# Attention scores as three rounded products from a ring of five key slots, instead of one full fp32 product from a ring of six

## The reference, cut to what matters

```
q, k = rms_norm(q, q_gain), rms_norm(k, k_gain)            # per head
s = einsum('bnqhd,bnkhd->bnhqk', q, k_band) * Dh ** -0.5   # chunk n sees chunks n-8 .. n
s = s + rel_bias(table, q_off, k_off)                      # distance clipped at +-128
s = where(valid, s, finfo.min)
o = einsum('bnhqk,bnkhd->bnqhd', softmax(s), v_band)
```

## Time and profile before

| | us |
|---|---|
| median of three timed runs | 1662.35 |
| the profiled execution, whole | 1657.24 |
| its span, first to last instruction | 1655.4 |
| TensorE busy in the span | 1589.1 (96%) |
| attention phase, from the first instruction to the last of `turn_o` | about 542 |
| one steady tile of attention (tiles 4 to 14) | 32.9 |

### The profile page before, as it was taken

One profiled execution on the slowest core, in us unless ns is written; L12 is line 12 of the kernel. 1 busy time (PEld: TensorE's weight loads), 2 busy tenths in 40 slices (PEclk: granted clock), 3 DMA queues, 4 the chain that ended last, 5 costly groups with the idle time before them and its releaser, 6 DMA issues. The chain is left out here.

```text
span 1655.4 us, 46730 instructions
## 1 busy us (share of the span) xinstructions
PE 1589.1 (96%) x20178; PEld 1297.6 (78%) x20178; DVE 807.3 (49%) x1152; ACT 878.9 (53%) x1833; POOL 518.7 (31%) x370
## 2 busy tenths in 40 slices
PE   6999999999999899999978999999999997999999
PEld 5788888888888788899976877777777775777787
DVE  5344444444444521121236677677676676533432
ACT  6566666666665521222246677677777675223420
POOL 3423121212130022122133466466465465400000
PEclk9999999999999999999998999999999999999999
DMA  6312211112113633533453223223223235286652
GB/s 244 106 61 93 72 58 50 67 60 73 52 50 122 210 110 115 163 97 100 125 161 111 62 77 106 63 76 106 63 77 104 64 98 185 84 303 224 210 176 76
DMA packets 136301, 184.43 MB, mean 111 GB/s; under 512 B 59153, under 2 KB 88337, under 8 KB 135842
## 3 DMA queue, kind: packets, MB, share of 16 engines
q1 hardware_dynamic: 129186, 170.83, 32.0%
q10 hardware_dynamic: 6912, 10.62, 1.8%
HBM read 122.42 MB, written 59.55 MB: 110 GB/s over the span
## 5 line engine op out<-in xcount | busy, mean ns | idle before, releaser
L677 PE MATMUL a_ps_proj<-a_w_hi,a_x_hi 128*128 128x512 f32 x384 | 155.8, 406 | 0.0
L677 PE MATMUL a_ps_proj<-a_w_hi,a_x_lo 128*128 128x512 f32 x384 | 150.2, 391 | 0.0
L677 PE MATMUL a_ps_proj<-a_w_lo,a_x_hi 128*128 128x512 f32 x384 | 149.6, 390 | 0.0
L587 DVE SCALAR_TENSOR_TENSOR a_stage<-a_ps_s,a_new_bias 128x256 f32<-128x256 f32 x64 | 27.2, 424 | 233.2 <-PE a_ps_s L704 233.2
L2481 PE MATMUL r_ps_gate<-gate_w_hi,gate_x_hi 128*128 128x512 f32 x272 | 119.0, 438 | 5.1 <-PEq L66 3.4
L1181 DVE SCALAR_TENSOR_TENSOR j_out<-j_ps,j_rest,j_part 128x512 f32<-128x512 f32 (+2 forms) x45 | 29.0, 644 | 177.4 <-ACT j_last_cols L1125 134.7
L362 POOL TENSOR_TENSOR a_xT<-a_xT,a_row 128x1024 f32<-128x1024 f32 x17 | 40.4, 2375 | 232.1 <-DMA a_row<-scratch_rstd 224.4
L2481 PE MATMUL r_ps_gate<-gate_w_lo,gate_x_hi 128*128 128x512 f32 x272 | 111.7, 411 | 0.0
L470 ACT ACTIVATE a_stage<-a_stage,a_small 128x640 f32<-128x640 f32 (+4 forms) x128 | 95.8, 752 | 0.9 <-DVE a_small L595 0.9
L1055 POOL TENSOR_TENSOR j_v_prev<-j_v_prev,shift_x 128x512 f32<-128x512 f32 x17 | 22.9, 1349 | 230.1 <-DMA j_v_prev<-scratch_v_raw 216.8
L704 PEld LDWEIGHTS a_ps_s<-a_kT,a_qT 64*128 64x128 f32 x592 | 59.8, 186 | 33.1 <-issue 28.0
(11 more groups left out here) (408 smaller groups left out, 4697.6 us busy)
## 6 DMA issues: line engine op xcount, KB each, us to landing
a_xT<-in_x_T SPq DMA_DIRECT2D x17, 512.0 KB, 3.3
scratch_xT<-a_xT SPq DMA_DIRECT2D x17, 512.0 KB, 2.6
raw<-scratch_xT SPq DMA_DIRECT2D x17, 512.0 KB, 5.4
scratch_gates<-r_gate_out SPq DMA_DIRECT2D x34, 256.0 KB, 3.2
z_gate<-scratch_gates SPq DMA_DIRECT2D x17, 512.0 KB, 3.8
a_x<-in_x_prompt SPq DMA_DIRECT2D x16, 512.0 KB, 3.5
o_x<-in_x_prompt SPq DMA_DIRECT2D x14, 512.0 KB, 4.8
out_y_prompt<-o_y SPq DMA_DIRECT2D x14, 512.0 KB, 2.9
```

The lines of the kernel that those rows point to most:

```text
L587: nc.vector.scalar_tensor_tensor(out=out[:, :, OLD:WIN], in0=ps_new, scalar=SCALE, in1=new_bias[:, 2 * c:2 * c + 2, :], op0=ALU.mult, op1= ...
L677: mm = nc.tensor.matmul(ps_proj[:], a[n % 2][:, k, :], w[:, k, g * AW:(g + 1) * AW], start=(k == 0 and i == 0), stop=(k == KT - 1 and i == 2))
```

## The change: what it does

- **Rounded halves.** Queries and keys are split: ScalarE writes a float32r rounding (`qT_hi`, `kT_hi`) where it wrote `qT` and `kT`, and VectorE writes the remainder (`qT_lo` by `qT_rest`, `kT_lo` by `kT_rest`, one pass over 128x512 each per tile). A score is then hi x hi + hi x lo + lo x hi, three float32r matmuls that add up in PSUM.
- **Ring of five.** Keys sit in five slots (`n % 5`) instead of six. Columns of the scores are ordered by slot of the ring, not by age: slots 0 to 2 ("main", 384 columns) in a bank per head, slots 3 and 4 ("side", 256 columns) of both heads in one bank. `ps_newest` now lies in the two main banks.
- **Order of the products.** First half: side of head 0 and main of head 1, three times in turn; then a wait of TensorE for the first half's last side product (`side_scored`); second half: side of head 1 and main of head 0, three times in turn. Tiles 0 to 2 have no side and no such wait.
- **VectorE reads by age.** `bias_and_max` takes the spans in order of age, cut where the ring wraps, where main meets side, and between far (three oldest) and near (two newest): 2 to 4 pieces in tiles 4 to 15 instead of 2. Far pieces add one mask shared by all heads, near pieces a bias per head. `scores` and the newest transposes now both wait for the count of all pieces (`biased`).
- **Waits on the turned bank.** `turn_qk` and `turn_o` write `ps_turn` only after the remainder has been read from it (`qkT_lo_ready`), and `scores` of a tile waits for `kT_rest`.
- **Smaller.** `k_out` is the same memory as the squares `qk_sq_out`, with a wait in `square_qk` for the stored k; the bias is loaded by one DMA, without waiting for a memset; q and k of the sample tile are written as plain float32. VectorE's reading of the first tile's q and k comes ahead of the loop.

```
...
-        ps_old = ps_s[:, 0:2 * OLD].rearrange("p (e n) -> p e n", e=2)
-        ps_new = ps_s[:, 2 * OLD:2 * WIN].rearrange("p (e n) -> p e n", e=2)
-        ps_newest = ps_s[:, 2 * WIN:2 * WIN + 2 * P].rearrange("p (e n) -> p e n", e=2)
+        main_banks = ps_s[:, 0:2 * 512].rearrange("p (e n) -> p e n", e=2)
+        ps_main, ps_newest = main_banks[:, :, 0:MAIN * P], main_banks[:, :, MAIN * P:(MAIN + 1) * P]
+        ps_side = ps_s[:, 2 * 512:3 * 512].rearrange("p (e n) -> p e n", e=2)
...
+        def side_steps(s):
+            return max(s - NP * MAIN, 0)
+
+        def spans(t, a, b):
+
+            found, j = [], a
+            while j < b:
+                slot = (t + 1 + j) % SLOTS
+                n = min(b - j, (MAIN if slot < MAIN else SLOTS) - slot)
+                found.append((j, j + n, ps_main[:, :, slot * P:(slot + n) * P] if slot < MAIN else ps_side[:, :, (slot - MAIN) * P:(slot - MAIN + n) * P]))
+                j += n
+            return found
+
+        def bias_steps(t):
+            lo = first_slot(t)
+            return [spans(t, lo, FIRST_NEAR), spans(t, max(lo, FIRST_NEAR), SLOTS)]
+
+        def biases(s):
+            return sum(NP * sum(map(len, bias_steps(t))) for t in range(s // NP)) + (s % NP and s % NP * sum(map(len, bias_steps(s // NP))))
 
...
             def square_qk(n, g):
                 act.wait_ge(proj_read, 3 * n + g + 1)
                 wait(act, qk_summed, 2 * n + g)
+                wait(act, k_stored, 16 * (n - 12))
                 nc.scalar.activation(qk_sq_out[:], qk[:, g, :], ACT.Square).then_inc(qk_sq, 1)
...
             def read_qT(n):
                 act.wait_ge(qk_turned, 2 * n + 1)
                 wait(act, scored, NP * (n - 1))
-                nc.scalar.activation(qT[n % 2][:], ps_turn[:].rearrange("p (c n) -> p c n", c=NP), ACT.Copy,
-                                     scale=consts[:, QK_GAIN_AT:QK_GAIN_AT + 1]).then_inc(qkT_ready, 1)
+                out = qT_hi[n % 2][:] if n < DEC else qT_sample[:]
+                nc.scalar.activation(out, ps_turn[:].rearrange("p (c n) -> p c n", c=NP), ACT.Copy,
+                                     scale=consts[:, QK_GAIN_AT:QK_GAIN_AT + 1]).then_inc(qkT_hi_ready, 1)
 
             def read_kT(n):
                 act.wait_ge(qk_turned, 2 * n + 2)
-                wait(act, scored, NP * (n - 1))
-                nc.scalar.activation(kT[:, :, n % RING, :], ps_turn[:].rearrange("p (c n) -> p c n", c=NP), ACT.Copy,
-                                     scale=consts[:, QK_GAIN_AT + 1:QK_GAIN_AT + 2]).then_inc(qkT_ready, 1)
+                wait(act, scored, NP * n)
+                out = kT_hi[:, :, n % SLOTS, :] if n < DEC else kT_sample[:, :, n % SLOTS, :]
+                nc.scalar.activation(out, ps_turn[:].rearrange("p (c n) -> p c n", c=NP), ACT.Copy,
+                                     scale=consts[:, QK_GAIN_AT + 1:QK_GAIN_AT + 2]).then_inc(qkT_hi_ready, 1)
 
             def exps(t, c):
...
+            def qT_rest(n):
+                dve.wait_ge(qkT_hi_ready, 2 * n + 1)
+                wait(dve, scored, NP * (n - 1))
+                nc.vector.scalar_tensor_tensor(out=qT_lo[n % 2][:], in0=ps_turn[:].rearrange("p (c n) -> p c n", c=NP),
+                                               scalar=consts[:, QK_GAIN_AT:QK_GAIN_AT + 1], in1=qT_hi[n % 2][:].bitcast(F32),
+                                               op0=ALU.mult, op1=ALU.subtract).then_inc(qkT_lo_ready, 1)
+
+            def kT_rest(n):
+                dve.wait_ge(qkT_hi_ready, 2 * n + 2)
+                wait(dve, scored, NP * n)
+                nc.vector.scalar_tensor_tensor(out=kT_lo[:, :, n % SLOTS, :], in0=ps_turn[:].rearrange("p (c n) -> p c n", c=NP),
+                                               scalar=consts[:, QK_GAIN_AT + 1:QK_GAIN_AT + 2], in1=kT_hi[:, :, n % SLOTS, :].bitcast(F32),
+                                               op0=ALU.mult, op1=ALU.subtract).then_inc(qkT_lo_ready, 1)
+
             def bias_and_max(t, c):
                 s, lo = NP * t + c, first_slot(t)
                 out = probs[s % 2]
                 wait(dve, p_turned, s - 1)
                 dve.wait_ge(scored, s + 1)
-                nc.vector.scalar_tensor_tensor(out=out[:, :, OLD:WIN], in0=ps_new, scalar=SCALE, in1=new_bias[:, 2 * c:2 * c + 2, :],
-                                               op0=ALU.mult, op1=ALU.add).then_inc(new_biased, 1)
-                if lo * P < OLD:
-                    nc.vector.scalar_tensor_tensor(out=out[:, :, lo * P:OLD], in0=ps_old[:, :, lo * P:OLD], scalar=SCALE,
-                                                   in1=old_bias[:, 2 * c:2 * c + 2, lo * P:OLD], op0=ALU.mult,
-                                                   op1=ALU.add).then_inc(old_biased, 1)
-                    dve.wait_ge(old_biased, s + 1 - NP)
-                dve.wait_ge(new_biased, s + 1)
+                masks = far_mask[:].rearrange("p (o n) -> p o n", o=1).broadcast_to([P, 2, FAR])
+                far, near = bias_steps(t)
+                for a, b, product in far:
+                    nc.vector.scalar_tensor_tensor(out=out[:, :, a * P:b * P], in0=product, scalar=SCALE, in1=masks[:, :, a * P:b * P],
+                                                   op0=ALU.mult, op1=ALU.add).then_inc(biased, 1)
+                for a, b, product in near:
+                    nc.vector.scalar_tensor_tensor(out=out[:, :, a * P:b * P], in0=product, scalar=SCALE,
+                                                   in1=near_bias[:, 2 * c:2 * c + 2, a * P - FAR:b * P - FAR],
+                                                   op0=ALU.mult, op1=ALU.add).then_inc(biased, 1)
+                dve.wait_ge(biased, biases(s + 1))
                 nc.vector.tensor_reduce(neg_max[s % 2], out[:, :, lo * P:WIN], AX_X, ALU.max, negate=True).then_inc(max_ready, 1)
 
             def invert(t):
@@ -625,6 +676,8 @@
             for g in range(2):
                 sum_qk(0, g)
...
+            qT_rest(0)
+            kT_rest(0)
...
                 sum_qk(t + 1, 1)
                 scale_qk(t + 1, 1)
+                if t + 1 < DEC:
+                    qT_rest(t + 1)
 
                 bias_and_max(t, 3)
+                if t + 1 < DEC:
+                    kT_rest(t + 1)
             split_shift_w()
...
                 pe.wait_ge(qk_scaled, 2 * n + g + 1)
-                wait(pe, qkT_ready, 2 * n + g)
+                wait(pe, qkT_hi_ready, 2 * n + g)
+                wait(pe, qkT_lo_ready, min(2 * n + g, 2 * DEC))
                 if g == 0:
                     wait(pe, out_ready, n - 2)
                 for c in range(NP):
@@ -692,26 +750,37 @@
...
             def scores(t, c):
                 s, lo = NP * t + c, first_slot(t)
                 if c == 0:
-                    pe.wait_ge(qkT_ready, 2 * t + 2)
+                    pe.wait_ge(qkT_lo_ready, 2 * t + 2)
                     if t == 0:
                         pe.wait_ge(proj_read, 3)
-                wait(pe, new_biased, s)
-                wait(pe, old_biased, s - NP)
+                wait(pe, biased, biases(s))
                 wait(pe, pT_ready, s - 1)
-
-                def product(e, a, b, out):
-                    half, r = slice(e * HD, (e + 1) * HD), ring(t, a)
-                    return nc.tensor.matmul(out, qT[t % 2][half, c, :], kT[half, c, r:r + b - a, :].rearrange("p j n -> p (j n)"),
-                                            start=True, stop=True)
-
-                product(0, SLOTS - 1, SLOTS, ps_new[:, 0, :]).then_inc(new_scored, 1)
-                cut = next((j for j in range(lo + 1, SLOTS - 1) if ring(t, j) == 0), SLOTS - 1)
-                for a, b in ((lo, cut), (cut, SLOTS - 1)):
-                    for e in (1, 0):
-                        if a < b:
-                            product(e, a, b, ps_old[:, e, a * P:b * P])
-                pe.wait_ge(new_scored, s + 1)
-                product(1, SLOTS - 1, SLOTS, ps_new[:, 1, :]).then_inc(scored, 1)
+                slots = min(t + 1, SLOTS)
+                main, side = min(slots, MAIN), max(slots - MAIN, 0)
+                q, k = (qT_hi[t % 2], qT_hi[t % 2], qT_lo[t % 2]), (kT_hi, kT_lo, kT_hi)
+
+                def main_product(e, i):
+                    half = slice(e * HD, (e + 1) * HD)
+                    return nc.tensor.matmul(ps_main[:, e, 0:main * P], q[i][half, c, :], k[i][half, c, 0:main, :].rearrange("p j n -> p (j n)"),
+                                            start=i == 0, stop=i == 2)
+
+                def side_product(e, i):
+                    half = slice(e * HD, (e + 1) * HD)
+                    return nc.tensor.matmul(ps_side[:, e, 0:side * P], q[i][half, c, :], k[i][half, c, MAIN:slots, :].rearrange("p j n -> p (j n)"),
+                                            start=i == 0, stop=i == 2)
+
+                for i in range(3):
+                    if side:
+                        first = side_product(0, i)
+                    main_product(1, i)
+                if side:
```

(27 more changed lines are left out.)

41 lines of the change are left out of this document (25 added, 16 removed).

## The result

The changed kernel takes 1666.76 us (median of 13 runs, 1661.37 to 1669.38), the kernel before 1657.37 (median of 13 runs beside it, 1655.33 to 1662.82). The ratio is 1.0049, with a 95% interval of 1.0037 to 1.0062: slower, as the interval leaves out 1, by an amount at the edge of the 0.5% that the forecast called no change. The profiled execution took 1663.36 us, its span 1661.4 (before 1657.24 and 1655.4).

What follows compares the result with a forecast made beforehand. TensorE's stream was taken to bound the attention phase. Score blocks +4.7 us and remainders at the start +1.5 us gave +6.2 us, from 1662.35 to 1668.5 us (0.37% slower), range 1656 to 1682.

Steps and rivals of the forecast that it cites:

- blocks, tiles 4 to 15: Score blocks on TensorE in tiles 4 to 15: 1.39 us instead of 1.28, 48 times, +5.1 us.
- block, tile 3: Score blocks in tile 3, with a side of 128 columns: 1.31 us against 1.07, four times, +1.0 us.
- blocks, tile 2: Score blocks in tile 2, no side and no wait: 1.06 us against 0.96, +0.4 us.
- blocks, tiles 0 and 1: Score blocks of the first two tiles: 0.69 us in tile 0 (-1.1), 0.79 to 0.80 in tile 1 (-0.7).
- first scores: Start, before the loop: first scores 1.5 us later than 40.04, bounds 0 and 2.2.
- The wait in mid-block: Between block halves, tiles 4 to 15: wait for head 0's side product ends at 0.675 us, 0.22 after its last column.
- The wait is nearly free: Rival, mid-block: next half begins when main of head 1 is done, block 1.24, -1.1 us in all, 1661.3; chance 0.15.
- Load 0.60: Tile 3's block: last side column at 0.378 us, load behind the wait at 0.60, block 1.31.
- Main of head 1 at 0.106, 0.279, 0.452, of head 0 to 0.964: Tile 2's block, no wait: these start times in us for main of head 1, main of head 0 until 0.964, block 1.06.
- The remainders: VectorE's passes, 0.69 us each: covered in the loop; before it, 0.75 with signal after each copy, +1.5 us.
- VectorE as the bound: Rival: pieces cost 0.2 us instead of 0.075, newest transposes come late, +3.6 us on top, 1672; chance 0.13.
- the other steps have the same slack: Newest transposes outside step 1: 0.5 us of transposes in between or step 1's slack (2.00 against 2.06), so no cost.

Runs made afterwards that it cites:

- single product: The changed kernel with one of the three float32r products instead of three, the rest of the scores left out; 1632.75 us in one execution.
- head-by-head kernel: Changed kernel reordered: side and main of head 0, main of head 1, the wait, then side of head 1; 1664.07 us in one execution.
- The run with the waits alone: Kernel before, with tile 0's two remainders computed into places nothing reads and TensorE waiting for them; 1660.06 us, ratio 1.0016.
- The kernel before with the longer wait alone: Kernel before, with the newest transposes waiting for every bias piece of the next step, not the newest slot's alone; 1656.64 us, ratio 0.9992.
- both edits: Changed kernel with main of head 0 ahead of the wait and the first tile's k transposed into the outputs' bank; 1654.09 us, ratio 0.9985.
- first-tile kernel: Changed kernel with the first tile's k transposed into the outputs' bank, not waiting for q's copy and remainder; 1661.24 us, ratio 1.0028.
- the four with k in the outputs' bank: Changed kernel with that k edit alone, plus main of head 0 ahead, plus filled start, plus later x statistics in tile 2: 1661.24, 1654.09, 1652.66, 1651.75 us.
- filled kernel: Changed kernel with main of head 0 ahead, first tile's k in the outputs' bank, and six projection products filling the start's gaps; 1652.66 us, ratio 0.9976.

## Why the prediction was right, and where it was not

The forecast was +6.2 us on the profiled span; the span grew by 6.0, the ratio of all runs says +8.1, and the medians of 13 lie 9.4 apart. The time itself, 1668.5, was only 1.7 too high because the shown median of three lay 5 us above that of 13 runs: a change forecast too small and a base too high cancel. Attention's last score block ends 9.0 us later (529.3, 538.3). That 6.0 is so near 6.2 is luck too: the 9.0 are met by 3.0 behind the phase that no instruction of the change touches. The mechanism of the largest term is right, four smaller ones are not. Term by term, in us:

| term | forecast | trace |
|---|---|---|
| blocks, tiles 4 to 15 | +5.1 | +5.7 |
| block, tile 3 | +1.0 | +1.4 |
| blocks, tile 2 | +0.4 | -0.9 |
| blocks, tiles 0 and 1 | -1.8 | -3.1 |
| first scores | +1.5 | +1.7 |
| low clock behind them | none | +2.5 |
| newest transposes and other gaps, tiles 0 to 3 | 0 | about +1.6 |
| after the attention phase | 0 | -3.0 |

*The wait in mid-block: right, mechanism and size.* Its load at 0.684 against a forecast of 0.675, the block 1.39 to 1.41 against 1.39, and with main of head 0 moved ahead the block fell to 1.22 as worked out. "The wait is nearly free" asked for 1.24 and is refuted by 1.40, and again by the single product's 0.81. By the Trainium skill, "TensorE: Matmul & The Clock Gate", section "The cost: per-tile semaphore tail" (25 ns, 4.7 per tile, 26.3 per increment), an estimate for one tile and one increment is 56 ns. The trace disagrees where TensorE waits for its own product: 0.22 to 0.24 us here, four times as much.

*Tile 3: the mechanism incomplete.* "Load 0.60" took the signal to follow the side product alone. It follows also what is issued ahead of it: 0.68, so tile 3 cost +1.4 instead of +1.0.

*Tiles 0 to 2: the step that failed.* "Main of head 1 at 0.106, 0.279, 0.452, of head 0 to 0.964" let head 0 begin only when head 1's third product had begun, in program order, without a wait that forced it. It put these tiles at -1.4 us; they gave -4.0. (The sum written for tile 1 is slipped besides: with six spacings of 0.12 it gives 0.91; its 0.79 to 0.80 is that of five.) In tile 1 the rows of the two heads are merged in pairs:

```profile
81.13 0.39 PE L764 MATMUL a_ps_s<-a_kT_hi,a_qT_hi 64*128 64x256 f32 x2
81.36 0.29 PE L764 MATMUL a_ps_s<-a_kT_lo,a_qT_hi 64*128 64x256 f32 x2
81.47 0.28 PE L764 MATMUL a_ps_s<-a_kT_hi,a_qT_lo 64*128 64x256 f32 x2
81.69 0.44 PE L807 MATMUL a_ps_out<-a_stage,a_v 128*64 128x128 f32 x4
```

Six products in the time of three: the second start of each pair lies 10 ns behind the first, though one head's product stands three places later in the program than the other's. With both halves running, tile 2 is 0.106 + 2 x 0.173 + 0.160 + 0.093 = 0.705 (0.735 measured). The head-by-head kernel shows the same in tiles 4 to 15. The Trainium skill, "TensorE: Matmul & The Clock Gate", section "The mechanism", says that matmuls start and end in program order, "strict FIFO". The trace disagrees on the start between halves of the rows: 10 ns apart instead of three products. It agrees on the order in which signals go out, 0.684 against 0.606 us in tile 3.

*The remainders.* In the loop they are covered as forecast: k's runs from 374.71 for 0.74 us (0.69 forecast), the next scores start at 377.10. At the start the size is right, +1.69 for "say 0.75" twice, and a consequence perhaps missed. A low clock behind them was no term, at 2.5 us the largest one left out. The run with the waits alone had it too, without any of the change's products; why it comes in one execution and not in another stays open. (VectorE was indeed free from 37.93, but that is a row of VectorE's timeline and not in the earlier trace rows.)

*VectorE as the bound: rightly refused, early tiles overlooked.* In step 1 of tile 10 its last bias ended 1.86 us after the block (forecast 1.90) and the newest transposes came 2.18 after (2.17), without a wait. But "the other steps have the same slack" was not true of tiles 1 to 3, which have few products between: there the newest transposes come up to 0.48 us later than before (tile 2, step 0), 1.6 us over the three tiles, which is the whole of that row. The kernel before with the longer wait alone has 1.5 of it.

*After the attention phase* no instruction changed. The 3.0 us are clock: from 530 us on the records show 34.0 us at the lower level before and 27.2 after, and half of the difference is 3.4. The time after the last block, over twelve profiled executions, varies from 1121 to 1129 us. Less half of the low-clock time in it, eleven lie at 1107 to 1110 (before 1109.0, changed kernel 1109.5) and one at 1114. So this row is not the change's, and the 8.1 to 9.4 us of the timed runs agree with the 9.0 of the attention phase. Why the clock falls there in one execution and not in another was not tried.

## What to carry to other kernels

- Work queued behind a wait pays for it whether it needs it or not. Put what is independent ahead: here three products moved ahead of the wait took 9.3 us off the score blocks, as much as the attention phase had lost in all.
- Where two halves of TensorE's rows have independent products, count each half's columns by itself, if the halves' products alternate or lie within three of each other in the program; the seventh product did not start with the first, but with the fourth. Count a signal from the last product issued ahead of it as well.
- A wait at a start can cost the clock behind it as well (2.5 us here), and time gained at a start can end in the next load: look there for the gain before calling an edit useless.

## What was not expected of the hardware

- Order: products on different halves of the rows overtake each other in starting (by two places, in tile 1 and in the head-by-head kernel), their signals do not (0.684 against 0.606 us by order alone).
- The load that ate the faster start reports 16 completions. With both edits, 15 of them came by 84.3 us and the last at 90.4; in the first-tile kernel by 85.8 and at 93.4. In the changed kernel it was 88.5 and 89.7. Transfers of instructions ran in that time in all of them; whether they hold up the last part was not tried.
- The clock at the start: with 1.7 to 1.8 us of idle time in all before the first scores it fell in one of six executions (before, its variant with the newest transposes, the four with k in the outputs' bank), with 3.3 to 3.6 us in five of six (all but the one-product kernel). So idle time there goes with the low clock but is not all of it. A single wait can do as well: in tile 2 of the kernel with both edits, 1.84 us without work were followed by 3.4 us at 0.5; the filled kernel waited 1.6 us there and kept 1.00.
